# One weight copy placed inside the norm, finer waits for the value weights, a later statistics step, and a last norm that writes x only

## The reference: what is computed

```python
for i in range(DEPTH):      # first stack, DEPTH = 2
    x = layer_norm(ALPHA * x + 0.5 * swiglu(x, ffn_w_in[i, 0], ffn_w_out[i, 0]), ...)   # norm 0
    x = layer_norm(ALPHA * x + token_mix(x, ...), ...)                                  # norm 1
    x = layer_norm(ALPHA * x + 0.5 * swiglu(x, ffn_w_in[i, 1], ffn_w_out[i, 1]), ...)   # norm 2
    ple = sigmoid(x @ ple_w_gate[i] + ple_b_gate[i]) * (p[i] @ ple_w_proj[i])
    x = layer_norm(ALPHA * x + ple, ...)                                                # norm 3
for l in range(DEPTH):      # second stack
    c_q, c_kv, k_r, gate_a, q_d, k_d, v_d, gate_b, gates = split(x @ w_in[l])
    y_a = dense attention of 8 heads (q from c_q, k and v from c_kv, rotary parts) * silu(gate_a)
    y_b = differential attention of 4 heads (q_d, k_d rotated, v_d) * silu(gate_b)
    merged = g1 * (y_a @ w_branch_a) + g2 * (y_b @ w_branch_b)
    x = layer_norm(ALPHA * x + merged @ w_out[l], ...)
```

## Time and profile before

| | us |
|---|---|
| median of 3 runs | 1704.04 |
| lowest and highest | 1701.02, 1707.57 |
| the profiled execution, its own time | 1704.24 |
| its span in the profile | 1702.5 |

### The profile page before, as it was taken

How to read it: one execution, slowest core, us unless ns; L and a number is a source line. 1 busy time by engine, 2 the same in 40 slices (tenths; PEclk the granted TensorE clock), 3 DMA queues, 4 the chain that set the end, 5 groups by cost and what they waited for, 6 DMA issues and landing times.

```text
span 1702.5 us, 32226 instructions
## 1 busy us (share of the span) xinstructions
PE 1628.7 (96%) x12958; PEld 1568.8 (92%) x12958; DVE 831.0 (49%) x1492; ACT 956.5 (56%) x1272; POOL 1263.4 (74%) x976
## 2 busy tenths in 40 slices
PE   9999999999999999999999999999988989999985
PEld 8999999999999989999999999999877979868885
DVE  3221377756221472213867572213767555586555
ACT  5435585266343674344853574345856875748855
POOL 7988867157989679988662479896785657775567
PEclk9999989999999999999999999999998999989998
DMA  7555443124655345555331245554443424443333
GB/s 297 205 187 184 173 147 127 50 100 152 218 177 197 125 173 206 198 180 187 130 132 67 74 150 201 195 179 167 158 149 107 142 99 149 158 147 121 121 113 118
DMA packets 37569, 262.24 MB, mean 154 GB/s; under 512 B 4160, under 2 KB 4544, under 8 KB 6336
## 3 DMA queue, kind: packets, MB, share of 16 engines
q1 hardware_dynamic: 36144, 257.74, 42.8%
q10 hardware_dynamic: 1296, 2.61, 0.5%
HBM read 259.28 MB, written 1.05 MB: 153 GB/s over the span
## 4 chain that ended last, share of the span: by engine, by line
POOL 60%; issue 27%; PE 7%; DVE 3%; ACT 2%; DMA 1%; POOLq 1%; SPq 0%; ACTq 0%
POOL wl L1339 60%; PE psum L746 2%; PE psum L748 2%; PE psum L747 2%; DMA raw<-wstream 1%; DVE arena L2474 0%; ACT arena L1804 0%; DVE arena L2389 0%; POOLq L1349 0%; ACT wh L1371 0%; DVE arena L2396 0%; PE psum L1270 0%; DVE arena L2394 0%; DVE arena L2387 0%; PE psum L1250 0%
## 5 line engine op out<-in xcount | busy, mean ns | idle before, releaser
L1339 POOL TENSOR_TENSOR wl<-raw,wh 128x512 fp32r<-128x512 f32 x972 | 1263.2, 1335 | 430.3 <-ACT wh L1371 422.0
L746 PE MATMUL psum<-xs,wh 128*128 128x256 f32 x1984 | 573.0, 289 | 1.7 <-issue 1.5
L748 PE MATMUL psum<-xs,wl 128*128 128x256 f32 x1984 | 563.6, 284 | 0.0
L747 PE MATMUL psum<-xs,wh 128*128 128x256 f32 x1984 | 561.6, 283 | 0.0
L1371 ACT ACTIVATE wh<-raw 128x2048 fp32r<-128x2048 f32 x240 | 458.5, 1914 | 134.9 <-PE psum L748 90.9
L746 PEld LDWEIGHTS psum<-xs,wh 128*128 128x128 f32 x1984 | 382.4, 193 | 7.5 <-issue 6.8
L747 PEld LDWEIGHTS psum<-xs,wh 128*128 128x128 f32 x1984 | 379.6, 191 | 0.8 <-issue 0.5
L748 PEld LDWEIGHTS psum<-xs,wl 128*128 128x128 f32 x1984 | 379.8, 191 | 0.0
L746 PE MATMUL psum<-arena_r,wh 128*128 128x256 f32 x1168 | 331.1, 284 | 4.2 <-DVE arena L2389 4.2
L747 PE MATMUL psum<-arena_r,wh 128*128 128x256 f32 x1168 | 328.5, 281 | 0.0
L748 PE MATMUL psum<-arena_r,wl 128*128 128x256 f32 x1168 | 328.4, 281 | 0.0
(11 more groups left out here) (327 smaller groups left out, 2041.5 us busy)
## 6 DMA issues: line engine op xcount, KB each, us to landing
raw<-wstream SPq DMA_DIRECT2D x242, 1024.0 KB, 4.8
cst<-consts SPq DMA_DIRECT2D x1, 1824.0 KB, 14.7
sm<-small ACTq DMA_DIRECT2D x3, 359.5 KB, 3.0
raw<-wstream SPq DMA_DIRECT2D x4, 256.0 KB, 5.6
out<-xT SPq DMA_DIRECT2D x4, 256.0 KB, 2.0
xT<-xt ACTq DMA_DIRECT2D x2, 256.0 KB, 4.5
xT<-xt ACTq DMA_DIRECT2D x1, 512.0 KB, 7.1
sm<-small ACTq DMA_DIRECT2D x3, 147.0 KB, 2.8
```

Of the source, the lines that this page charges most:

```text
L746: mm(o, a[0], b[0], start=start, stop=False, skip_group_check=shared)
L747: mm(o, a[0], b[1], start=False, stop=False, skip_group_check=shared)
L748: return mm(o, a[1], b[0], start=False, stop=stop, skip_group_check=shared)
L1339: return nc.gpsimd.tensor_tensor(wl[:, s, quarter(q)], raw[:, s, quarter(q)], wh[:, s, quarter(q)].bitcast(F32), ALU.subtract)
```

## The change

It does five things:

1. `ln_act` gets a `middle`: the copy behind the second lead slot is made before block 7 of norms 0, 1 and site 4, and before block 3 of norm 3, instead of after the norm.
2. The values take their weights by input block, 4 tiles at a time.
3. The statistics of norm 3 stand behind lead step 3 instead of step 1.
4. The last norm makes `xT` only: no `xs`, no low part. The 3 slots of zeros at the end go (their loads, copies and subtractions).
5. The small constants of a layer that doesn't exist are not loaded any more, nor waited for, at the end of either stack.

```diff
-SLOTS = DEPTH * (L1 + L2) + SPLIT
+SLOTS = DEPTH * (L1 + L2)
-LEAD_STAT = {0: 0, 1: 1, 3: 1, 4: 0}
+LEAD_STAT = {0: 0, 1: 1, 3: 3, 4: 0}
...
-                wa = [v.rearrange("p (k n) -> p k n", k=4) for v in w.take(16)]
-                wb = [v.rearrange("p (k n) -> p k n", k=4) for v in w.take(16)]
                 o = []
                 for k in range(KD):
-                    wv = [v[:, k % 4, :] for v in (wa if k < 4 else wb)]
+                    wv = w.take(4)
...
                 def next(self):
                     n = self.s + SPLIT + self.before
+                    self.s += 1
+                    if n + self.li * len(self.slots) >= SLOTS:
+                        return
                     act.wait_ge(loaded[n % RING], (self.li * (len(self.slots) // RING) + (n // RING + 1)) * 16)
                     A(wh[:, n % SPLIT, :], raw[:, n % RING, :], ACT.Copy).then_inc(high_ready, 1)
-                    self.s += 1
...
                 then()
                 for n in range(KD):
+                    if n == middle[0]:
+                        middle[1]()
...
-                    A(xs[:, n, 0, :], r, ACT.Identity, bias=b, scale=g).then_inc(*h_.tick(*key(1, n)))
+                    if h_ is not None:
+                        A(xs[:, n, 0, :], r, ACT.Identity, bias=b, scale=g).then_inc(*h_.tick(*key(1, n)))
                     A(xT[:, n, :], r, ACT.Identity, bias=b, scale=g).then_inc(*x_.tick(*key(1, n)))
...
+                    def middle():
+                        if s < 2:
+                            feed("lead", s, LEADS - 1)
+                        elif s == 3:
+                            after("lead", 3, LEADS - 1)
...
-                           lambda k, *n: (s,) + n, lambda n: (p1("g", s * 8 + n, 1), p1("b", s * 8 + n, 1)), then, taken if s < 2 else None)
+                           lambda k, *n: (s,) + n, lambda n: (p1("g", s * 8 + n, 1), p1("b", s * 8 + n, 1)), then, (3 if s == 3 else KD - 1, middle), taken if s < 2 else None)
...
+                if li == DEPTH - 1:
+                    return
                 wait(xrd, 3, KD - 1)
                 wait(usl, 3, KD - 1)
                 act.dma_start(sm1[:], small1[li + 1]).then_inc(small1_in, 16)
...
+                def middle():
+                    if li < DEPTH - 1:
+                        feeds[DEPTH + li + 1]("lead", 4, LEADS - 1)
...
-            act.wait_ge(small1_in, (DEPTH + 1) * 16)
-            act.wait_ge(small2_in, (DEPTH + 1) * 16)
...
                 def low(n):
+                    if l_ is None:
+                        return
                     dve.wait_ge(*x_.at(li, *key(1, n)))
```

More of the change, by code:

```diff
@@ L632, in hybrid @@
         xrd2 = sig("x2_ready", range(KD))
-        xhi2 = Signal(nc, ctx, "x_high_ready", [[(n,) for n in range(KD)]] * DEPTH, base=(4 * DEPTH + 1) * KD, sem=xhi.sem)
-        xlo2 = Signal(nc, ctx, "x_split", [[(n,) for n in range(KD)]] * DEPTH, base=(4 * DEPTH + 1) * KD, sem=xlo.sem)
+        xhi2 = Signal(nc, ctx, "x_high_ready", [[(n,) for n in range(KD)]] * (DEPTH - 1), base=(4 * DEPTH + 1) * KD, sem=xhi.sem)
+        xlo2 = Signal(nc, ctx, "x_split", [[(n,) for n in range(KD)]] * (DEPTH - 1), base=(4 * DEPTH + 1) * KD, sem=xlo.sem)
         yah = sig("ya_high_ready", range(4))
@@ L1391, in __call__, with ln_act @@
                         self.next()
-            def ln_act(li, full, stat_bank, stat_key, m_, v_, s_, n_, x_, h_, key, gb, then, taken=None):
+            def ln_act(li, full, stat_bank, stat_key, m_, v_, s_, n_, x_, h_, key, gb, then, middle, taken=None):
                 act.wait_ge(*full.at(li, *stat_key))
@@ L1844, in then @@
                         feed("y", KD - 1)
+                def middle():
+                    if li < DEPTH - 1:
+                        feeds[DEPTH + li + 1]("lead", 4, LEADS - 1)
                 def taken(n):
                     return usd.at(DEPTH, 4, n) if n < KD - 1 else full2.at(li + 1, "lead", 4, LEADS - 1)
-                ln_act(li, full2, bank2("stat"), ("stat",), lnm2, lnv2, lns2, lnn2, xrd2, xhi2,
-                       lambda k, *n: n if k else (0,), lambda n: (p2("g", n, 1), p2("b", n, 1)), then, taken if li < DEPTH - 1 else None)
+                ln_act(li, full2, bank2("stat"), ("stat",), lnm2, lnv2, lns2, lnn2, xrd2, xhi2 if li < DEPTH - 1 else None,
+                       lambda k, *n: n if k else (0,), lambda n: (p2("g", n, 1), p2("b", n, 1)), then, (KD - 1, middle), taken if li < DEPTH - 1 else None)
                 assert feed.s == L2
+                if li == DEPTH - 1:
+                    return
                 wait(xrd2, KD - 1)
-                if li < DEPTH - 1:
-                    act.wait_ge(*usl.at(DEPTH, 4, KD - 1))
+                act.wait_ge(*usl.at(DEPTH, 4, KD - 1))
                 act.dma_start(sm2[:], small2[li + 1]).then_inc(small2_in, 16)
@@ L2653 @@
         stream += [slots(np.concatenate([bb, ba], axis=1).reshape(-1, P, P)), slots(tiles(a["w_out_2"][l]))]
-    stream += [np.zeros((SPLIT, P, SLOT), np.float32)]
     wstream = np.concatenate(stream)
@@ L2663, in spread @@
         return np.broadcast_to(v.reshape(1, -1), (P, v.size))
-    small1 = np.zeros((DEPTH + 1, P, N1), np.float32)
-    small2 = np.zeros((DEPTH + 1, P, N2), np.float32)
+    small1 = np.zeros((DEPTH, P, N1), np.float32)
+    small2 = np.zeros((DEPTH, P, N2), np.float32)
     for l in range(DEPTH):
```

2 lines of the change are left out of this document (1 added, 1 removed).

## The result

| | before | after |
|---|---|---|
| median, us | 1705.8 (4 runs) | 1692.49 (4 runs) |
| lowest and highest | 1701.02, 1708.37 | 1692.15, 1696.4 |
| profiled execution, its own time | 1704.24 | 1696.4 |
| its span | 1702.5 | 1694.6 |

The ratio is 0.9923 with a 95% interval of 0.99 to 0.9945: 13.1 us faster, with 9.4 to 17 in the interval. The forecast was 1689, the range 1682 to 1697.

The account below looks back on a forecast made before the run. It took TensorE, busy for 1628.7 of 1702.5 us, as the bound. Terms 0 (norms 0, 1, site 4) + 2.0 + 5.7 + 2.5 + 5.2 = 15.4, so 1704.2 became 1688.8, given as 1689 us; range 1682 to 1697.

Parts of the forecast that it names:

- norm 3, first layer: First stack's norm 3: later statistics fill PE's wait for the residual's sum and `by_input` starts earlier; 2.0 us, bounds 0 and 3.4.
- second stack, first layer, with its norm 3: Earlier norm 3, raw slot and values, limited by DVE's chain to the rotations; 5.7 us, bounds 2.2 and 7.3.
- second stack, second layer: Raw-slot wait and DVE's wait for PE go, less half clock before `kup`; 2.5 us, bounds 0.5 and 5.2.
- the end: After the last matmul: without `xs` and low parts the last `xT` comes earlier; 5.2 us, bounds 4.3 and 5.6.
- five slower low parts: Norm 3: low parts of x on DVE beside POOL's work, 0.45 each; all on the path make 2.2 us.
- 1.37 + 2.59 - 1.5: Second stack, second layer: raw-slot wait plus DVE's wait for PE, less lower clock at the new wait; 2.5 us.
- Rotations start 3.55 + 2.16 = 5.7 earlier, and so does everything behind `kup`: Second stack, first layer: earlier Sqrt (3.55) and no DVE wait for PE (2.16) move rotations and later work 5.7 us.
- rival B: Second stack: with POOL ahead, DVE's rotations run alone and `kup` never waits; 21.5 us gained, 1683 us; chance 0.10.
- the 0.97 that I had named as the sign of a wrong prediction: Whole span: a TensorE clock below 0.97 would show the prediction wrong.
- A (given back): PE's waits and half clock move, norm 3 gains 0; 7.1 to 8.1 us gained, 1696 to 1697; chance 0.17.
- C: Slower: copy before block 3 adds waits in `by_input`, clock stays half; needs 48 us of it; chance 0.03.
- D: Little but the end works: raw slots no earlier, norm 3 gains nothing; 7.6 us gained, 1697 us; chance 0.05.

Follow-up runs that it names:

- experiment 5: The changed kernel with the statistics of norm 3 behind lead step 1 again; median 1693.85 us, ratio 0.9942 to the kernel before.
- experiment 1: The changed kernel with whole value slots, norm 3's statistics behind step 1 and copies behind the norms, so only the end changed; median 1699.03 us, ratio 0.9955.
- experiment 3: The changed kernel with the value weights taken by whole slots again; median 1694.38 us, ratio 0.9933 to the kernel before.
- experiment 9: The changed kernel with two ScalarE copies of slots held back behind `kup`'s reads, to keep POOL quiet during the rotations; median 1695.8 us, ratio 0.994.
- experiment 4: The changed kernel with the copy behind the second lead slot after the norm at all sites again; median 1698.81 us, ratio 0.9959 to the kernel before.
- experiments 7: The changed kernel with the rotary key's sum on DVE (L2396) moved behind the four groups of rotations; median 1686.84 us, ratio 0.9897.
- 8: The changed kernel with `pqd` between the products of `kd` and two groups of rotations ahead of the `cqs` work on DVE; median 1687.0 us, ratio 0.9893.
- 10: The changed kernel with two of three DVE instructions per group of the query's rotary part moved behind the maxima of heads 0 to 3; median 1690.76 us, ratio 0.9917.
- experiment 11: The changed kernel with the moves of experiments 7, 8 and 10 together, the key's rotary sum behind head 0's probabilities; median 1674.48 us, ratio 0.9815.
- 12: The kernel of experiment 11 with the value weights taken by whole slots again; median 1683.99 us, ratio 0.989 to the kernel before.

## Why the prediction was right, and where it was off

The time lies 3.5 us above the forecast and inside the range. Part by part, from the profiles (marks in the same profile, so the 4.8 us of the first layer stay out):

| term | predicted | read |
|---|---|---|
| norm 3, first layer | 2.0 | 1.8 |
| second stack, first layer, with its norm 3 | 5.7 | 4.5 |
| second stack, second layer | 2.5 | 0.5 |
| the end | 5.2 | 5.7 |
| sum | 15.4 | 12.5 |

The second and third rows end at the first maxima; the sum stands beside 13.1 measured. In this one pair of profiles two places outside the table cancel: 1.1 us gained between the second layer's token mix and its norm 2, and 1.0 lost behind the last layer's first maxima, both in code that the change leaves alone but for a copy's place.

**Norm 3.** In the first layer right, and for the reason given: `by_input` starts 3.3 us earlier (3.4 predicted), the copy before block 3 costs 1.2 (1.2 predicted), and experiment 5 takes the statistics back and the whole gain goes. The leads end 4.5 us earlier; I had written 4.7, where my own terms (2.0 + 0.7 + 1.75) make 4.45. The 2.2 us that five slower low parts would have made on the path are not there but for the 0.33. What I had not seen is that block 0 was later in before only because of the half clock behind the waits: in experiment 5's second layer and experiment 1's first, with the waits but no half clock, only 0.2 is lost. The gain is that of a clock stretch which doesn't come in every execution.

**Second stack, first layer.** The chain of DVE was the right one. Counted from the first matmul behind norm 2 of the second layer, the rotations start 5.3 us earlier (5.7 predicted), and the last of them ends 5.2 earlier. The nearness is in part luck. Norm 3 gave 3.1 instead of 2.2, and DVE's work from the reciprocal to the rotations took 14.5 us instead of 13.1, since its two-input operations came to lie beside POOL's (L2396 3.25, before 2.28): 3.1 + 1.45 + 2.16 - 1.4 = 5.3. Behind the rotations 0.7 goes to the clock between `kup` and `pqa` (5.7 us instead of 5.0). PE's waits before `kup` make 5.6, where I had named 3 to 5.

**Second stack, second layer: the mis-sized term.** I had taken 1.37 + 2.59 - 1.5. The first two are there: rotations start 3.6 earlier. The 1.5 for the clock was 2.1 (5.6 instead of 3.5 from the last rotation to `pqa`). What I left out is 1.5 more: the rotations took 13.48 us instead of 11.99, because all of them now lie beside POOL, which was busy for 13.5 of these 13.5 us and for 10.0 of the 12.0 before. (In the first layer they took 13.4 before already.) The step that failed is "Rotations start 3.55 + 2.16 = 5.7 earlier, and so does everything behind `kup`", carried over to this layer; it takes the rotations' length as fixed. I had the row for it, a low part of 0.44 alone and 0.89 beside POOL, and used it for norm 3 and in rival B with the opposite sign: there POOL being ahead was to leave DVE alone. Experiments 3 and 9 decide it: the four groups take 10.7 us with two of them alone, 9.1 with three alone, 13.5 beside POOL. The Trainium skill ("SBUF — State Buffer", section "🔬 SBUF: two separate sides") says that a DVE operation with two SBUF inputs and a GpSimd operation shut each other out for a whole instruction; the runs agree (0.68 alone, 1.18 and 1.65 beside POOL), and also in what it leaves out: L2402, with one input from PSUM, stays at 0.68 in all of them.

**The clock.** It ended at 0.975, as before, above the 0.97 that I had named as the sign of a wrong prediction. That the new wait is paid in clock again holds; the windows right behind the last of the three waits, in after:

```profile
1278.40:1284.00 5.60, 5.55 (x15) 3.63 (x16) 0.00 (x0) 2.50 (x4) 2.36 (x2) 0.55 0.41 139
1284.00:1290.00 6.00, 6.00 (x22) 3.23 (x21) 5.85 (x6) 2.37 (x2) 4.84 (x4) 0.74 0.18 71
```

PE is busy, and the clock is 0.55 and then 0.74.

**The end.** 5.2 up to the last `xT` (14.49 to 9.28; predicted 4.8 + 0.3), and 0.5, not 0.1, for what lies behind it.

**The rivals.** A (given back) is half true: the waits did move and the second layer gave back nearly all, but norm 3 gained. What I gave for it, that every long wait but those of the end was followed by half clock, isn't so in before itself: the clock stays at 1.00 behind the waits of 1.88 (until 578.92), 2.85 (until 1546.12) and 3.11 (until 1624.95). B didn't come: `kup` waits. Its picture is that of experiment 3, where POOL is ahead, two groups run alone and `kup` waits 0.43. C needed 48 us of half clock more; the profile has 3.4 more outside the end. D had "the raw slots come no earlier", and the reciprocal comes 1.45 us earlier in both layers.

**Which edit earned it.** The end, 5.7 (experiment 1: 7.7, with 4.1 to 11.4). The statistics, 1.8 in the first layer and 0.2 in the second against experiment 5. The early copies, nothing that the profile shows, and 6.1 ± 4.8 by the time (experiment 4). The values edit, 1.7 to 2.9, neither clear of nothing. How the gain of the second stack (second stretch: 3.9) is shared between the copies, the values and the statistics isn't shown.

**What stays open.** Experiment 4's 6 us; what ends the waits that the profile puts down to the issue; and whether experiments 7, 8 and 10 are worth more together than one by one. By the ratios they make 4.4, 5 and 1 alone and 18 together, but the sum of three such differences is known to some ±13; in the second stretch they make 8.9 + 4.2 + 3.2 = 16.3 alone and 18.4 together. Single executions differ by up to 5 us through stretches of half clock in layers that no edit touched; a gain of one or two microseconds at one place can't be told in the total and was read by its stage alone.

## What to carry to other kernels

Before you price the removal of a wait, follow the waiting engine's next partner to its own next instruction; if that partner has two or three pieces of work in its queue ahead of the next hand-over, the wait moves from one to the next (here from the values to `kup`, and from `kup` to the first head), until all of them are gone. The same edit can be worth 2 us, not to be told from nothing, while another engine is late and 7 to 13 once it is not, so a null result for an edit is to be tried again after the next bound is gone. Starting work earlier isn't free if it then runs beside an engine that holds it up: look at each instruction's duration alone and beside that engine before you move it. And before you credit an edit with a difference between two profiles, look at how far kernels with the same code at that place differ.

## What the hardware showed that I had not expected

- The same DVE instruction of 128x512 with two inputs from SBUF takes 0.68 us with POOL idle, and 1.18 or 1.65 beside POOL's subtraction of 1.34; with one input from PSUM it takes 0.68 in both cases. Three groups of rotations differ by 4.3 us by this alone (5.9 and 10.2, experiment 9).
- Half clock comes behind short waits too, and not by a fixed amount. After's first layer has 10.2 us of it at 249.20, behind a wait of 1.26; before's has 3.4 there behind one of 0.50, and 10.2 in its own second layer behind 2.02, in the same code. The waits may not be all of it: right behind each of them stand 32 matmuls of one column (L916), and no run separates the two. With no wait in the stage, in experiment 11, the clock was 1.00 in both layers; with one of 4.2 us, in 12, it was 0.95.
- Half clock comes without any wait as well. Before's PE has no wait from 15.0 to 247.2, and yet its clock falls at 223.7, behind matmuls of 8 columns (L896, from 221.11 on), with PE busy throughout:

```profile
222.00:223.70 1.70, 1.70 (x17) 1.70 (x17) 1.67 (x4) 1.70 (x3) 1.70 (x2) 1.00 0.01 5
223.70:226.00 2.30, 2.30 (x13) 2.30 (x13) 1.29 (x6) 2.27 (x6) 2.30 (x3) 0.51 0.93 306
```

  It is 6.8 us of half clock in before, 3.4 in after, none in experiment 3. Such stretches are where executions of one kernel differ: the code from the first layer's `wab` to the first matmul behind its norm 2, which only a copy's place sets apart, took 357.1 to 361.8 us over the kernels here, and four executions of after differ by 4.2 us in their spans (1690.4 to 1694.6).
